# GpSimd's remainders of weight slabs in pieces of 512 columns instead of 1024, in a transformer block kernel on one core

## The reference, cut to what matters

```python
def swiglu_ffn(x, norm, w_gate, w_up, w_down):
    h = rms_norm(x, norm)
    return (jax.nn.silu(h @ w_gate) * (h @ w_up)) @ w_down
# first_block, twice: ffn1; h @ w_in (11 projections); three attention branches;
#   three w_branch and w_out; ffn2
# second_block, once: context: h @ w_in_2 (part), conv, scan -> states
#   p = h @ w_in_2; conv_rows, silu, ssd_bidir, fourier_mix
#   x + gm * rms_norm(concatenate([fourier_mix(u), y]) @ w_out_2) ; swiglu
```

## Time and profile before

| | us |
|---|---|
| median of three runs | 1617.53 |
| the profiled execution's own time | 1617.06 |
| its span (first to last instruction) | 1615.3 |
| TensorE busy (matmuls) | 1599.0 (99%) |
| VectorE busy | 1291.9 (80%) |
| ScalarE busy | 927.8 (57%) |
| GpSimd busy | 213.0 (13%) |

### The profile page before, as it was taken

The page is one execution under the profiler, slowest core; times in us unless marked ns, Lnnn a source line. Parts: engine busy times, 40 slices in busy tenths (PEclk is TensorE's granted clock), DMA queues, the critical chain, the costliest instruction groups (busy, mean ns, idle before and its releaser), DMA issues.

```text
span 1615.3 us, 29921 instructions
## 1 busy us (share of the span) xinstructions
PE 1599.0 (99%) x13140; PEld 1534.8 (95%) x13140; DVE 1291.9 (80%) x1464; ACT 927.8 (57%) x1113; POOL 213.0 (13%) x125
## 2 busy tenths in 40 slices
PE   8999999999999999999999999999999999899998
PEld 8999988999999999999987899999999989899998
DVE  7887878687888987997878688786899688796655
ACT  7554656685465555555555686455556567654544
POOL 1000100000040001110000000032332368600000
PEclk9999999999999999999999999999999999999999
DMA  7667644444556765667754444555554344335551
GB/s 292 230 263 276 253 182 159 155 157 157 211 221 250 258 256 206 263 245 276 263 188 175 157 146 158 187 212 191 200 187 182 131 155 184 131 131 198 194 189 73
DMA packets 48264, 320.73 MB, mean 199 GB/s; under 512 B 5372, under 2 KB 8188, under 8 KB 10632
## 3 DMA queue, kind: packets, MB, share of 16 engines
q1 hardware_dynamic: 47992, 318.81, 53.7%
q10 hardware_dynamic: 144, 0.02, 0.0%
HBM read 317.74 MB, written 1.07 MB: 197 GB/s over the span
## 4 chain that ended last, share of the span: by engine, by line
PE 91%; DVE 5%; ACT 1%; POOL 1%; DMA 1%; issue 0%; SPq 0%; DVEq 0%; ACTq 0%
PE ps L1235 26%; PE ps L1237 25%; PE ps L1236 25%; PE ps L1433 3%; PE ps L1435 3%; PE ps L1434 3%; DVE wlo L1903 2%; PE ps L1447 1%; POOL wlo L567 1%; PE ps L1458 1%; DMA raw<-in_w_dram 1%; PE ps L1714 1%; DVE tmp L1903 1%; DVE qkA L1903 1%; DVE pre L2512 1%; PE ps L1661 0%
## 5 line engine op out<-in xcount | busy, mean ns | idle before, releaser
L1903 DVE TENSOR_TENSOR wlo<-raw,whi 128x2048 fp32r<-128x2048 f32 (+2 forms) x255 | 583.9, 2298 | 93.5 <-ACT whi L686 90.4
L686 ACT ACTIVATE whi<-raw 128x2048 fp32r<-128x2048 f32 (+1 forms) x264 | 500.0, 1906 | 208.4 <-DMA raw<-in_w_dram 207.9
L1235 PE MATMUL ps<-h1hi,whi 128*128 128x256 f32 x1792 | 500.1, 279 | 3.5 <-DVE wlo L1903 3.5
L1237 PE MATMUL ps<-h1lo,whi 128*128 128x256 f32 x1792 | 496.1, 277 | 0.0
L1236 PE MATMUL ps<-h1hi,wlo 128*128 128x256 f32 x1792 | 496.1, 277 | 0.0
L1235 PEld LDWEIGHTS ps<-h1hi,whi 128*128 128x128 f32 x1792 | 336.9, 188 | 7.4 <-DVE h1lo L1962 3.1
L1237 PEld LDWEIGHTS ps<-h1lo,whi 128*128 128x128 f32 x1792 | 336.7, 188 | 0.0
L1236 PEld LDWEIGHTS ps<-h1hi,wlo 128*128 128x128 f32 x1792 | 336.6, 188 | 0.1
L1235 PE MATMUL ps<-hid_hi,whi 128*128 128x256 f32 x880 | 243.8, 277 | 0.0
L1236 PE MATMUL ps<-hid_hi,wlo 128*128 128x256 f32 x880 | 243.1, 276 | 0.0
L1237 PE MATMUL ps<-hid_lo,whi 128*128 128x256 f32 x880 | 243.1, 276 | 0.0
(11 more groups left out here) (366 smaller groups left out, 2601.1 us busy)
## 6 DMA issues: line engine op xcount, KB each, us to landing
raw<-in_w_dram SPq DMA_DIRECT2D x288, 1024.0 KB, 4.8
from_start<-decay_dram SPq DMA_DIRECT2D x3, 768.0 KB, 4.2
raw<-in_w_dram SPq DMA_DIRECT2D x8, 256.0 KB, 5.8
c_rows<-in_c_rows_dram SPq DMA_DIRECT2D x2, 1024.0 KB, 10.1
relbias<-in_relbias_dram SPq DMA_DIRECT2D x2, 1024.0 KB, 8.5
pv<-in_pv_dram SPq DMA_DIRECT2D x2, 641.0 KB, 7.7
xT<-in_x_dram SPq DMA_DIRECT2D x4, 256.0 KB, 4.8
raw<-in_w_dram SPq DMA_DIRECT2D x2, 512.0 KB, 6.6
```

What stands on the lines that cost most here:

```text
L686: act.activation(whi[:, slot, c], raw[:, slot, c], ACT.Copy).then_inc(hi_done[slot], 1)
L1235: pe.matmul(out, w_hi, hi, start=start, stop=False, skip_group_check=skip)
L1237: return pe.matmul(out, w_hi, lo, start=False, stop=stop, skip_group_check=skip)
L1903: return dve.tensor_tensor(out, a, b, op)
```

## The change

GpSimd's `cut_lo` goes over the slab in quarters of 512 columns instead of halves of 1024. The operation, its operands, the wait ahead of the first piece and the counter raised by the last are the same. The slab in `DT_SLABS` takes its last two quarters. GpSimd issues 74 such operations instead of 37; no other engine's program is touched.

```diff
@@ -563,7 +563,8 @@
         def cut_lo(g):
             slot = PLACE[g] % NS
             pool.wait_ge(hi_done[slot], SPLITS[g])
-            for c in (slice(0, SLAB // 2), slice(SLAB // 2, SLAB))[1 if g in DT_SLABS else 0:]:
+            for q in range(2 if g in DT_SLABS else 0, 4):
+                c = slice(q * SLAB // 4, (q + 1) * SLAB // 4)
                 ins = pool.tensor_tensor(wlo[:, slot, c], raw[:, slot, c], whi[:, slot, c].bitcast(F32), ALU.subtract)
             ins.then_inc(lo_done[slot], 1)
```

## The result

Measured over 20 executions, the changed kernel takes **1620.16 us** at the median (1618.23 to 1625.87) against 1617.53 us before. The ratio, taken over the means, is **1.0023, with a 95% interval of 1.0015 to 1.0030**; the two medians alone would give 1.0016. It is slower by 0.23%, some 3.7 us, where 1.0 us and no measurable change were forecast; the median lies inside the range given, near its upper end.

The account below looks back on a forecast made before the run. TensorE bounds the kernel, except near 1390, where GpSimd's output slabs set the end. Four terms of 0.28 us make 1.12, taken as +1.0 after the clock: 1617.53 to 1618.5 us, called same; range 1616.9 to 1620.6.

Parts of the forecast that it names:

- The price of a cut: Each extra cut of a GpSimd slab costs 0.14 us, 0.28 per slab; GpSimd works 5.2 us more over 37 cuts.
- The rival by which cuts are free: A cut and a turn cost nothing and the gap doesn't move: 0.0, 1617.5 us; chance 0.08.
- The price of a turn: A 256-column VectorE operation that slips in at a boundary between GpSimd operations costs GpSimd 0.14 us.
- Step (1): GpSimd's chain starts at 1372.81 after a 0.69 us wait for ScalarE, which absorbs up to 0.69 us of earlier losses.
- Steps (2), (3): Slabs WOUT20 and WOUT20 + 1: +0.28 us each; the latter ends at 1386.51 instead of 1385.95, still hidden from TensorE.
- Step (4): VectorE's wlo for WOUT20 + 3 follows WOUT20 + 1, ending at 1388.65 instead of 1388.09; only moves TensorE's idle time forward.
- Step (5): WOUT20 + 2: cuts +0.28, two more norm turns +0.28; done 1.12 us later in all, TensorE's gap 2.86 to 3.98.
- The clock: TensorE's half-clock stretch after the gap gives a little back, so the 1.12 us loss is taken as 1.0.
- my two clock cases: After the longer gap: two slow stretches, +2.5 us (1620.0), or the low stretch wholly idle, -0.4 (1617.1); chance 0.13 for both.
- The other slabs: Elsewhere slabs are 0.28 us later, two in a row 0.56, hidden by leads; last context slab 0.9 later, 0.2 lead left.
- The rival of turns in this stage: Context stage: VectorE gets in between quarters more often than counted, TensorE waits at 1199.2; +2.9 to +4.4 us, chance 0.10.
- The rival on the slower side: The context-stage rival: uncounted VectorE turns between quarters delay the slab; +2.9 us, or +4.4 (1621.9) with the clock; chance 0.10.

Follow-up runs that it names:

- experiment 7: Single GpSimd waits for its own completion: quarters except output projection, one ahead of xw_x, 0.9997; changed kernel, two (ahead of xw_x, after z_gate(2)), 1.0004 of the kernel before.
- experiment 3: Quarters everywhere but in the output projection, against the kernel before, run again to profile a long execution: 1623.48 us.
- experiment 1: The changed kernel once more, nothing altered, for a second profile: 1620.96 us.
- experiment 4: Quarters only in some slabs, against the kernel before: six context slabs 1.0004; nine projection slabs 1.0019; the projection slabs without the last two 1.0001.

## Why the prediction was wrong

**What bounds the kernel: right.** All that the change cost lies where the earlier trace rows put GpSimd on the path, and just ahead of it.

**The price of a cut: right.** 0.14 us; GpSimd worked 4.8 us more against 5.2 said. The rival by which cuts are free has fallen.

**The price of a turn: right.** 0.14 forecast, 0.16 measured where turns were taken (experiment 7).

**Step (1), the start absorbs what came before: right.** The quarters of WOUT20 start at 1374.86, beside 1375.29 in the earlier trace rows.

**Steps (2), (3): right.** WOUT20 + 1 is the first four of the eight quarters and ends at 1381.06 + 4 x 1.24 = 1386.0 (1386.51 said, with a later start); TensorE didn't wait for it.

**Step (4) is the one that failed.** It has VectorE's wlo go at the end of WOUT20 + 1 and take 3.3 us (1385.34 to 1388.65); it took 8.00. The rule behind it, "at each end of a GpSimd operation a waiting VectorE operation goes first", was read from five cases in one execution, all with halves. In the changed kernel the wlo did not get in at WOUT20 + 1's end but four ends later, in both profiled executions. The rule was true of the strings that I could see (up to nine operations) and I took it for a rule of all strings, while the change makes just these longer. The prediction even has the sentence that more ends let more operations of VectorE in; for such strings the runs show the opposite. The rule was also too narrow on what takes part: zex has a single input, and it waits for GpSimd's operations like those with both inputs in SBUF (experiment 3). How the failure shifts the price: TensorE waits for VectorE's slab, 1.85 us more instead of 1.12.

The moment of asking alone doesn't explain it. The wlo was asked for 0.36 us into a quarter and was passed over; 0.37 us into one with two gaps added, and was let in. zex, asked for 0.32 us into the first xw_x, was passed over (experiment 3), and 0.34 us in, in experiment 1, it was not. That it plays a part isn't excluded. Nor is the length of the string a fixed bound: at 11, the wlo got its turn in the profiled execution of the output slabs alone, asked for 0.20 us into its quarter.

**Step (5): its picture was right for a kernel in which VectorE gets its turns** (experiment 7, three operations of 1.17 to 1.37 us, gap 3.71, medians +1.5 us and the ratio 0.6 us, against +1.0 said), but not for this one: there the three had no turns to take.

**The clock: mis-sized.** I let it give 0.1 us back; it took 0.94 more. "A second slow clock stretch" was named as what would show me wrong, and its rival (+2.5 us, 1620.0) gives the time of the short executions, but by luck in part: the gap was 4.7 us and not 3.98. But the length of the gap doesn't fix the outcome: over the profiled executions, TensorE's wait for the output slabs was followed by no half clock at 2.6 and 2.7 us, by 3.41 us of it at 2.4, 2.5, 2.6, 2.7, 2.9, 3.0 and 3.7, and by 6.83 us at 2.9, 3.0, 3.7 and 4.7. So my two clock cases were right to stand as rivals, but the forecast itself, one stretch at 3.98, had no better ground than they. The Trainium skill (TensorE: Matmul & The Clock Gate, Part 1) holds that idle gaps of TensorE bring the half clock; these runs agree in that every slow stretch here stands behind a gap, but not every gap has one.

**The other slabs: the context stage right, the projection stage missed.** The last context slab went as computed. GpSimd's, VectorE's and TensorE's lines, beside the earlier trace rows:

```profile
1190.11 8.05 POOL L568 TENSOR_TENSOR wlo<-raw,whi 128x512 fp32r<-128x512 f32 x4
```
```profile
1191.35 2.66 DVE L1904 TENSOR_TENSOR wlo<-raw,whi 128x2048 fp32r<-128x2048 f32 x1
1193.93 1.79 DVE L1904 TENSOR_TENSOR hid_lo<-t_hid,hid_hi 128x512 fp32r<-128x512 f32 x1
```
```profile
L1218 PEldq EVENT_SEMAPHORE  x1: 51/51/51, 1198.9 to 1198.9; - x1
```

The slab is done at 1198.16, TensorE asks at 1198.9: 0.7 us of lead (0.2 said), hid_lo 1.79 (1.8 said). The rival of turns in this stage has fallen, with 0 of 11 long for the context slabs alone. But for the projection slabs I asked only whether *they* would be late, against leads of microseconds. They weren't. Late was an unchanged VectorE operation behind them, a case that no rival held. Undoing two of these slabs undid the long executions (experiment 4), which are 1.6 us of the mean, a term that the sum had at nothing.

**The chances.** The rival on the slower side asked for the right thing, a turn given where none was counted, and had the wrong sign: VectorE gets its turn too seldom, not too often.

**Shown and argued.** Shown: the passing over, twice at the output and twice at xw_x; that the share of long executions rises with the length of the string (8, 12, 20) and falls back with 0.07 us of idle time ahead of the operation in which VectorE asks; that undoing the two slabs ahead of xw_x undoes the long executions. At the output the evidence is thinner: with a string of 11 made of quarters the wlo was passed over in two of three profiled executions, with idle times in none of three. Only argued is why. The Trainium skill (GPSIMD Engine Reference, section 2.1) says that consecutive GpSimd instructions are no barrier between its cores: each starts its share of the next one when it has finished its share of this one. If the cores drift apart over a long string, one of them is always reading, and there is no moment at which VectorE finds the ports free; a wait for the own completion would bring them together. Everything above agrees with that, but no record shows single cores, and no run takes the drift away in another way. The Trainium skill (SBUF — State Buffer, section "Who interferes with whom") has the second of two such operations blocked until the first is done; here it was blocked until the fifth was done.

## What to carry to other kernels

Where VectorE must get in between GpSimd operations on SBUF, count how many of them follow one another without idle time, over unchanged ones too: a finer cut lengthens that string, and a VectorE operation can then be passed over until GpSimd runs out. One wait of GpSimd for its own completion ahead of the place cost 0.07 us here, and with it the long executions went (0 of 11); moving the contended work to one engine at the tight place was better still (0.9987). And where such an outcome falls now one way and now the other, a single profiled execution shows one side of it, so the spread of the times comes first.

## What the runs showed of the hardware

- A VectorE operation with its operands in SBUF took 8.00 us instead of 2.3, and a one-input operation of 512 columns took 6.43 and 7.40 instead of 1.2. Beside the first, GpSimd kept its pitch of 1.24 us for each quarter.
- With strings of 6 to 8 operations ahead of xw_x some 5% of the executions were long (9 of 189), with 12 some 43% (25 of 58), with 20 all (6 of 6).
- A GpSimd operation of 512 columns has a pitch of 1.24 us, of 1024 one of 2.335; of 256, with eight in 5.59 us, 0.70.
- The half clock behind a gap of TensorE came as 3.41 us, as 6.83 or not at all, for gaps of the same length (2.6: none and 3.41; 3.0 and 3.7: 3.41 and 6.83). Behind gaps of 1.3 us none was seen.
